# Hybrid decoder step: paged keys turned on VectorE in 32x32 blocks, and the projection tiles reordered around it

## The reference

```python
k_full = k_pages[pt_b[:n_full * ppb]].reshape(n_full, M_BLOCK, M_HEADS, M_DH)
means = jnp.mean(k_full.astype(jnp.float32), axis=1).swapaxes(0, 1)
idx, valid = moba_select(qh, means, n_full_q, k_sel)      # best 3 of 4 blocks of 256
...
return moba_core(qh, kg, vg, valid, k_own, v_own, own_mask)   # softmax over them and the own tokens
```

## Time and profile before

| What | Value |
|---|---|
| Median of 3 runs | 1973.92 us (1972.58 to 1979.55) |
| Profiled execution, span from first to last instruction | 1972.4 us |
| Median less span | 1.5 us |
| TensorE busy | 1951.0 us, 99% |
| VectorE busy | 1269.6 us, 64% |
| ScalarE busy | 881.4 us, 45% |
| POOL busy | 145.1 us, 7% |
| Granted TensorE clock | 0.999 of full speed |
| DMA traffic | 267 MB, mean 135 GB/s |

### The profile page before, as it was taken

One profiled execution on the slowest core, in us unless ns is written; L12 is line 12 of the kernel. 1 busy time (PEld: TensorE's weight loads), 2 busy tenths in 40 slices (PEclk: granted clock), 3 DMA queues, 4 the chain that ended last, 5 costly groups with the idle time before them and its releaser, 6 DMA issues. The chain is left out here.

```text
span 1972.4 us, 40938 instructions
## 1 busy us (share of the span) xinstructions
PE 1951.0 (99%) x16779; PEld 1829.6 (93%) x16779; DVE 1269.6 (64%) x2022; ACT 881.4 (45%) x1423; POOL 145.1 (7%) x231
## 2 busy tenths in 40 slices
PE   9999999999999999999999999999999999999999
PEld 8968978998999999999998798799899999999999
DVE  6475413347765988988674743143686658889876
ACT  4365522323534454655434754233334344555544
POOL 0001120012000000000000012200120000000000
PEclk9999999999999999999999999999999999999999
DMA  6327683246244343333343277812552442433332
GB/s 214 124 69 221 203 283 103 86 148 205 89 153 132 86 132 97 97 108 91 102 157 131 86 215 236 286 52 91 171 163 90 157 139 71 136 104 107 87 113 83
DMA packets 262059, 267.12 MB, mean 135 GB/s; under 512 B 14026, under 2 KB 225138, under 8 KB 261362
## 3 DMA queue, kind: packets, MB, share of 16 engines
q1 hardware_dynamic: 241522, 190.69, 31.3%
q0 software_dynamic: 20224, 73.68, 11.5%
q10 hardware_dynamic: 128, 0.15, 0.0%
HBM read 239.43 MB, written 25.03 MB: 134 GB/s over the span
## 5 line engine op out<-in xcount | busy, mean ns | idle before, releaser
L1999 DVE TENSOR_TENSOR WL<-RAW,WH 128x2048 fp32r<-128x2048 f32 (+2 forms) x76 | 161.1, 2120 | 93.0 <-ACT WH L1428 93.0
L856 PE MATMUL PS<-XH,WH 128*128 128x272 f32 x960 | 203.3, 293 | 0.6
L856 PE MATMUL PS<-XL,WH 128*128 128x272 f32 x960 | 198.3, 288 | 0.0
L856 PE MATMUL PS<-XH,WL 128*128 128x272 f32 x960 | 198.0, 287 | 0.0
L1334 PE MATMUL PS<-KQ,CH 128*128 128x272 f32 x1088 | 158.3, 288 | 1.4 <-DVE KQ L2552 1.4
L1428 ACT ACTIVATE WH<-RAW 128x2048 fp32r<-128x2048 f32 (+2 forms) x84 | 149.8, 1783 | 21.8 <-PE PS L856 19.1
L856 PEld LDWEIGHTS PS<-XH,WH 128*128 128x128 f32 x960 | 150.5, 188 | 7.8 <-issue 5.2
L836 PE MATMUL PS<-WH,XH 128*128 128x256 f32 x512 | 152.1, 297 | 0.0
L856 PEld LDWEIGHTS PS<-XL,WH 128*128 128x128 f32 x960 | 150.9, 188 | 0.0
L856 PEld LDWEIGHTS PS<-XH,WL 128*128 128x128 f32 x960 | 150.3, 189 | 0.0
L1334 PEld LDWEIGHTS PS<-KQ,CH 128*128 128x128 f32 x1088 | 145.0, 188 | 2.2 <-issue 2.2
(11 more groups left out here) (464 smaller groups left out, 5266.8 us busy)
## 6 DMA issues: line engine op xcount, KB each, us to landing
RAW<-in_w_in SPq DMA_DIRECT2D x94, 512.0 KB, 4.7
RAW<-in_w_gu SPq DMA_DIRECT2D x128, 256.0 KB, 3.8
PG<-in_cache_k SPq DMA_DIRECT2D x64, 256.0 KB, 3.3
PG<-in_cache_k POOLq DMA_DIRECT2D x64, 256.0 KB, 3.4
RAW<-in_w_down SPq DMA_DIRECT2D x64, 256.0 KB, 4.0
RAW<-in_w_gu SPq DMA_DIRECT2D x24, 512.0 KB, 4.6
PG<-in_cache_v SPq DMA_DIRECT2D x44, 256.0 KB, 3.9
PG<-in_cache_v POOLq DMA_DIRECT2D x44, 256.0 KB, 4.2
```

The lines of the kernel that those rows point to most:

```text
L856: last = pe.matmul(PS[:, 2 * pair + h, 0:HALF], w[:, i, c0:c0 + P], block[:, h * HALF:(h + 1) * HALF], start=first and i == 0 and a == 0, ...
L1999: dve.tensor_tensor(WL[:, slot, 0:n], RAW[:, slot, 0:n], WH[:, slot, 0:n].bitcast(F32), ALU.subtract).then_inc(lo_ready, 1)
```

## The change

Key pages are no longer turned on TensorE. Each page is fetched by four DMAs of 64 KB. DMA g takes features 128g to 128g + 127 of all 128 tokens and puts token 32c + k on partition 32g + k, for the four c side by side. One VectorE instruction (`dve.transpose`) then turns every 32x32 block of a page number's four pages (128 x 2048) in place. The contraction over features now takes four products with 32 features of each of the four bands, so the sample queries have their columns in another order (`sample_pairs`), and `QB` is made by eight-head masked products on VectorE (`query_block`) from a new constant `qmask`. `KTT`, its copies and POOL's memset of `QB` go.

There are four key buffers (two `PG`, a part of `XT`, and `PGK` where the attention operand `MT` was) and three of them serve the values. `rqk` is cut: its first unit (`rqa`) stays in the attention stage, with tile 3 now there and tile 4 ahead of the first scores; the `rv` tiles fill the key stage; the other three units (`rqb`) fill the value stage. Scores and probabilities of the two groups use different PSUM banks.

```diff
+    PAGE_BUFS = (PG[:, 0], PG[:, 1], XT[:, 4:8, 0:SEQ], PGK[:])
@@ pages
+            v = r - V_STEP
+            if r == 2:
+                hold(eng, xt_kept, lay * 16 + 16)
+            elif r == 3:
+                hold(eng, s_done, lay * 16 + 16)
+            elif 4 <= r < V_STEP:
+                hold(eng, sc_done, scores_done(lay, r - 4))
+            elif 0 <= v < 3:
+                hold(eng, sc_done, scores_done(lay, V_STEP - 4 + v))
             for b in seqs:
-                if r >= V_STEP + 3:
-                    hold(eng, pvs_page, lay * 64 + 4 * (r - V_STEP - 3) + b + 1)
...
-                elif r >= 2:
-                    hold(eng, kt_done, lay * 64 + 4 * (r - 2) + b + 1)
+                if v >= 3:
+                    hold(eng, pvs_page, lay * 64 + 4 * (v - 3) + b + 1)
                 e = (r // N_PAGES % 2 * GRP + b) * N_PAGES + r % N_PAGES
                 page = eng.value_load(PTAB[0:1, e:e + 1], min_val=0, max_val=cache_k.shape[1] - 1)
...
+                src = src.rearrange("o n (c k) h d -> k (o n c) (h d)", k=32)
+                for g in range(4):
+                    dst = key_buf(r)[32 * g:32 * g + 32, b, :].rearrange("k (c d) -> k c d", c=4)
+                    eng.dma_start(dst, src[:, :, g * P:(g + 1) * P]).then_inc(arrived[r % 4], 16)
@@ SP
-                for at_r, name, j, col in ((2, "rqk", 2, C_RQ), (6, "rqk", 3, C_RQ), (11, "rv", 0, C_RV),
-                                           (14, "rv", 1, C_RV), (20, "rv", 2, C_RV), (23, "rv", 3, C_RV),
-                                           (27, "br_att", 0, C_GA)):
+                for at_r, name, j, col in ((4, "rv", 1, C_RV), (7, "rv", 2, C_RV), (10, "rv", 3, C_RV),
+                                           (14, "rqb", 0, C_RQ + UC), (18, "rqb", 1, C_RQ + UC),
+                                           (21, "rqb", 2, C_RQ + UC), (25, "br_att", 0, C_GA)):
@@ TensorE, end of the prompt attention
                 if s == 16:
-                    turn_keys(0, (0,))
+                    token_part("rqa", 3, kk[:4])
                 if s:
                     turn_probs(s - 1)
             attend(14)
-            turn_keys(0, (1,))
+            token_part("rqa", 3, kk[4:])
             attend(15)
@@ key_scores
-                pe.wait_ge(kt_act, lay * 64 + 4 * q + 4)
+                pe.wait_ge(kt_turned, lay * 16 + q + 1)
...
-                for hp in range(4):
+                for e in range(4):
                     for b in range(GRP):
-                        last = pe.matmul(PS[32 * b:32 * b + 32, 4 + p // 4, (p % 4) * P:(p % 4 + 1) * P],
-                                         QB[:, hp, (g * GRP + b) * 32:(g * GRP + b + 1) * 32],
-                                         KTT[q % 2][:, b, hp, :], start=hp == 0, stop=hp == 3)
+                        keys = key_buf(q)[:, b, :].rearrange("p (c e k) -> p c e k", c=4, e=4)[:, :, e, :]
+                        last = pe.matmul(PS[32 * b:32 * b + 32, (4, 0)[g] + p // 4, (p % 4) * P:(p % 4 + 1) * P],
+                                         QB[:, e, (g * GRP + b) * 32:(g * GRP + b + 1) * 32],
+                                         keys, start=e == 0, stop=e == 3)
@@ TensorE, key and value stage
+            token_part("rqa", 4, kk)
+            for q in range(V_STEP):
+                for f in value_rows(q):
+                    token_part("rv", f, kk)
+                key_scores(q)
+                if q == 11:
+                    turn_sample_probs(0)
+            for i in range(V_STEP):
+                g, p = divmod(i, N_PAGES)
+                if i == 0:
+                    token_part("rv", 4 * TT - 1, kk)
+                for f in late_rows(i):
+                    token_part(*rq_tile(f), kk)
+                if i == 4:
+                    turn_sample_probs(1)
+                attend_sample(g, p)
+                if i == 9:
+                    to_columns(0)
@@ VectorE
+            def query_block(j):
+                dve.wait_ge(tr_done, lay * 16 + j + 1)
+                q = PS[:, QK_BANKS[j % 3][1], 0:NS].rearrange("p (b q) -> p b q", q=DEC_L)
+                w = cl("qmask")[:, j // 2 * 8:j // 2 * 8 + 8]
+                dve.tensor_tensor(QB[:, j, :].rearrange("p (b h q) -> p b h q", b=DEC_B, q=DEC_L),
...
+            def turned(r):
+
+                dve.wait_ge(page_in[r % 4], key_landings(lay, r))
+                dve.wait_ge(page_in_b[r % 4], key_landings(lay, r))
+                dve.transpose(key_buf(r), key_buf(r)).then_inc(kt_turned, 1)
@@ VectorE, prompt attention (after the scaling of step s and row_max(s + 2))
+                if s in (8, 10, 12):
+                    turned(s // 2 - 4)
@@ VectorE, key stage
             rotated(2)
-            for q in range(NG * N_PAGES):
+            split_at(U0["rv"])
+            rotated(3)
+            turned(3)
+            rotated(4)
+            for q in range(V_STEP):
+                if q in (1, 5, 9, 13):
+                    split_at(U0["rv"] + (q + 3) // 4)
+                if 4 <= q + 3 < V_STEP:
+                    turned(q + 3)
                 if q == N_PAGES:
                     select(0)
```

More of the change, by code:

```diff
@@ L430, in diag, with key_buf, slot_total, key_landings @@
         return bass.AP(a.tensor, a.offset + 0, [list(a.ap[0]), [256, 4], [36, 8], [1, 4]])
-    def own_query(hp, z):
-        return QB[64 * z:64 * z + 64, hp, :].rearrange("p (b c) -> p b c", c=32)[:, :, 8 * hp + 4 * z:8 * hp + 4 * z + 4]
-    def page_slot(r):
-        if r < V_STEP:
-            used = [r % 2 == q % 2 for q in range(r)]
-            return r % 2, PG[:, r % 2], sum(used), V_STEP // 2 + len(range(r % 2, V_STEP, 3))
-        slot, before = (r - V_STEP) % 3, (r - V_STEP) // 3
-        keys = V_STEP // 2 if slot < 2 else 0
-        buf = PG[:, slot] if slot < 2 else PGE[:]
-        return slot, buf, keys + before, keys + len(range(slot, V_STEP, 3))
+    def key_buf(q):
+        return PAGE_BUFS[q % 4]
+    def slot_total(slot):
+        return V_STEP // 4 * KEY_PIECES + 32 * len(range(slot, V_STEP, 3))
+    def key_landings(lay, q):
+        return lay * (slot_total(q % 4) if q % 4 < 3 else V_STEP // 4 * KEY_PIECES) + (q // 4 + 1) * KEY_PIECES
+    def value_slot(lay, v):
+        slot = v % 3
+        return slot, PAGE_BUFS[slot], lay * slot_total(slot) + V_STEP // 4 * KEY_PIECES + (v // 3 + 1) * 32
+    def scores_done(lay, q):
+        return lay * 18 + q + 1 + (q >= N_PAGES)
     def row_bank(name, f):
-        if name == "rqk" and f < 2:
+        if name == "rqa" and f < 2:
             return 1, slice(f * UC, (f + 1) * UC)
-        return (3, 6)[f % 2], slice(0, UC)
+        if name == "rqa" and f == 3:
+            return 2, slice(0, UC)
+        return (3, 6)[(T0[name] + f - T0["rqa"]) % 2], slice(0, UC)
     QK_BANKS = ((4, 5), (6, 7), (2, 3))
@@ L463, in out_pair, with value_rows, late_rows @@
         return (0, 2, 6, 4, 0)[t]
-    def value_tiles(g, p):
-        step, out = g * N_PAGES + p, []
-        for r in ((0, 1) if step == 0 else (step + 1,) if step + 1 < 4 * (TT - 1) else ()):
-            u, i = divmod(r, TT - 1)
-            out += [u * TT, u * TT + 1] if i == 0 else [u * TT + 1 + i]
-        return out
-    def filler(q):
-        return q + 3 if q < N_PAGES else q + 5
+    def value_rows(q):
+        return [q - 1 + u for u in range((q + 3) // 4 - (q % 4 == 1), (q + 3) // 4 + 1)] if q else []
+    VALUE_STEPS = (1, 2, 3, 5, 6, 7, 8, 10, 11, 12, 13, 14)
+    def late_rows(i):
+        if i not in VALUE_STEPS:
+            return []
+        n = VALUE_STEPS.index(i)
+        return [TT + n // 4 * TT] * (n % 4 == 0) + [TT + n // 4 * TT + 1 + n % 4]
     def out_bank(h):
@@ L832, in token_part @@
                 if t == TT - 1:
-                    last = sample_part(u, bank, (0, 1) if len(ks) == KT else (ks[0] // 4,))
+                    last = sample_part(slot, bank, (0, 1) if len(ks) == KT else (ks[0] // 4,))
                 for k in ks if t < TT - 1 else ():
@@ L878, in unit2, with transposes @@
                 feature_tile(tile + 1, 2 * slot + 1, slot, UC, P, kts, rhs)
-            def transposes(srcs, base, pairs, between):
+            def transposes(srcs, base, pairs, between, sample=None):
                 w = len(pairs)
@@ L892, in transposes @@
                         else:
-                            pe.matmul(PS[:, bank, 0:NS], src(t), STK, start=True, stop=True).then_inc(tr_done, 1)
+                            rows = src(t) if sample is None else sample(j)
+                            pe.matmul(PS[:, bank, 0:NS], rows, STK, start=True, stop=True).then_inc(tr_done, 1)
                     between(j)
@@ L927, in sample_rkv, with sample_columns @@
                     last.then_inc(rs_done, 1)
-            transposes([rows_of(QK, j) for j in range(8)], 0, QK_BANKS, sample_kv)
+            def sample_columns(j):
+                return QK[:, TT - 1, j * P:(j + 1) * P]
+            transposes([rows_of(QK, j) for j in range(8)], 0, QK_BANKS, sample_kv, sample_columns)
```

(10 more changed lines are left out.)

323 lines of the change are left out of this document (135 added, 188 removed).

## The result

The change makes the kernel slower: 1985.62 us median of 12 runs (1978.34 to 1989.96) against 1973.96 of 12 runs before (1972.42 to 1979.55), a ratio of 1.0055 with a 95% interval from 1.0043 to 1.0066. The forecast was 1950, with a range up to 1976.

What follows compares the result with a forecast made beforehand. TensorE, busy 99%, bounds the kernel before; key-page supply was to bound the changed key stage. Saving 2.0 there and 9.7 in the value stage, 23.4 us over both layers, takes the 1972.4 span to 1949.0, so 1950 (range 1926 to 1976).

Steps and rivals of the forecast that it cites:

- Transposes off TensorE, turning at 2.3 us: All 512 TensorE transposes go, at most 56 us in both layers; VectorE turns each page in 2.3 us instead.
- Rival B: On VectorE, turning takes twice the split, 4.6 us, costing 7 us a layer: 1964 us; chance 0.13.
- Attention stage: Three turnings inserted in VectorE's attention loop cost 4.0 us (bounds 0 and 6.9); last attention product ends at 154.1.
- Page 0's release: Key stage start: page 0 is scored by 161.5 us, and only then may page 4 be issued.
- Supply of 5.8 us a page: Key stage: the queues issue a page in 5.8 us (bounds 5.0 and 7.3), over TensorE's 4.1; scores end at 236.8.
- break-even of 6.8 us a page: Key-page issue: the change turns from gain to loss at 6.8 us a page.
- Bandwidth has room as well: Key stage DMA: 512-byte rows move 297 GB/s at a full share, while a page with its weights asks 233.
- D: Key stage: issuing a piece costs POOL 0.756 us, a page 7.2, 17 us more a layer: 1984 us; chance 0.08.
- E: Key-page DMA: pieces writing only 32 partitions run at half of 297 GB/s, 40 us more a layer: 2030; chance 0.05.
- Value stage: Value stage takes 65 us instead of 74.7, saving 9.7 a layer (bounds 1.5 and 11.3).
- Rival C: The value stage is bound by its transfers and saves only 1.5 us: 1966 us; chance 0.14.
- Slower: Whole kernel slower by more than the 10 us a measurement can tell, the cases D and E; chance 0.13.

Runs made afterwards that it cites:

- e5: Changed kernel with the turnings of pages 0 to 2 moved from VectorE's attention loop to behind its last step: 1975.55 us.
- e9: e5 with TensorE scoring pages 0, 1 and 2 directly behind the last attention product, ahead of the fifth retention tile: 1958.16 us.
- e6: Changed kernel with VectorE's block selection of group 0 moved ahead of the turning of page 9, from behind that of page 11: 1989.0 us.
- e7: Changed kernel with 12 idle TensorE products ahead of the wait for each turned page from page 4 on, except page 8: 1997.02 us.
- e8: Changed kernel with four of the 16 pieces of each of pages 4 to 15 issued by ScalarE's queue: 1982.91 us.
- e2: Changed kernel with one 256 KB DMA per key page of a sequence, in 512-byte runs, without placing the feature bands: 1953.55 us.
- e11: Changed kernel with two 128 KB pieces per key page of a sequence, whole rows to 64 neighbouring partitions each, without placing the feature bands: 1967.27 us.
- e12: Changed kernel with two 128 KB pieces per key page of a sequence, half the columns to all 128 partitions each, without placing the feature bands: 1944.4 us.
- e16: e11 with one piece writing the even and the other the odd partitions, instead of the first and last 64: 1947.43 us.
- e13: e9 plus ScalarE's queue sharing the pieces of pages 6 to 15 (1949.64 us), then block selection moved ahead of page 10's turning: 1944.48 us.
- e3: Changed kernel with its four 64 KB pieces cut by blocks of 32 keys, each writing all 128 partitions and a quarter of the columns: 2080.9 us.

## Why the prediction was wrong

- **Transposes off TensorE, turning at 2.3 us.** Right: 512 instructions fewer, and 2.308 us for a turning. That is what the split takes for as many elements (2.29). The trace agrees so far with the Trainium skill's page "Vector Engine (DVE) Microarchitecture Reference", section 3.8, by which a transposing pass sustains one element per cycle per lane. Rival B is out.
- **Attention stage.** The mechanism was right, the term 2 us short: 156.1 instead of 154.1. The three insertions were priced at 4.0; e5, which takes them out of the loop, ends at 150.4, so they cost 5.7. VectorE's small gaps took nothing back.
- **Page 0's release.** Forecast 161.5, found 166.3 (164.93 + 1.40). Of the 4.8 us, 2 are the attention's. The pause before the fifth tile was forecast well, at 3.3 us, and found at 3.42, although the rotation that it was reckoned from ends at 151.09 (150.80 + 0.29) and not at 150.80. The rest is a thing that the forecast had nowhere. Behind that pause, in the fifth tile, TensorE's products stand 0.21 us apart instead of 0.12, the 1.2 GHz level instead of 2.4 (granted clock 0.50 from 160 to 164 us, 1.00 from 150 to 156 and again from 167 to 171). Windows, then the timeline:

```profile
150.00:156.00 6.00, 6.00 (x64) 5.31 (x60) 0.00 (x0) 1.45 (x2) 0.00 (x0) 1.00 0.55 166
160.00:164.00 4.00, 4.00 (x21) 4.00 (x21) 2.99 (x9) 2.27 (x2) 0.00 (x0) 0.50 0.02 4
167.00:171.00 4.00, 4.00 (x60) 3.73 (x56) 2.89 (x7) 1.19 (x3) 2.53 (x5) 1.00 0.46 131
```

```profile
159.54 0.55 PE L868 MATMUL PS<-WH,XH 128*128 128x256 f32 x1 [3.42 <-ACT EA L1468]
159.89 0.41 PE L869 MATMUL PS<-WL,XH 128*128 128x256 f32 x1
160.10 0.41 PE L870 MATMUL PS<-WH,XL 128*128 128x256 f32 x1
...
167.35 0.28 PE L869 MATMUL PS<-WL,XH 128*128 128x256 f32 x1
167.47 0.28 PE L870 MATMUL PS<-WH,XL 128*128 128x256 f32 x1
```

  The tile took 5.4 us (159.54 to 164.93) instead of 3.08. Page 0's scores then took 1.40 us instead of 1.01. In the kernel before, the pause at this place was 1.51 us and the clock stayed at 1.00 (150 to 156 us). In the changed kernel the clock fell again later: from 196 to 200 us TensorE was busy 1.50 us of 4, and from 200 to 205 the granted clock was 0.68. e9, in which the fifth tile waits only 0.65 us and page 0 is released first, shows what an early release is worth: 17.4 us.
- **Supply of 5.8 us a page.** This is the step that failed: 12 x 5.8 from 161.5, and 1.9 for the landing. The suspect was right, but its terms were too small. The scores of layer 0 end at 251.5 instead of 236.8, 14.7 us late:

| Term | Forecast | Found | Adds |
|---|---|---|---|
| Page 0's release | 161.5 | 166.3 | 4.8 |
| From the release to POOL's first piece of page 4 | 0 | 1.3 | 1.3 |
| Issue of twelve pages on POOL | 69.6 | 75.6 | 6.0 |
| From the end of the issue to the last landing | 1.9 | 4.65 | 2.7 |
| Turning, last scores, own keys | 3.8 | 3.65 | -0.1 |

  The issue was too small because a page takes POOL 6.05 without pauses (the forecast had 5.5 for POOL) and because of the pauses. The one of 2.40 us comes after the first piece that POOL issues for page 14. It is as long and at the same piece in e5, e6, e7 and e9, so TensorE's waits, which differ there, do not make it; what does was not found. By the forecast's own break-even of 6.8 us a page, POOL's 6.30 would still have left a small gain, so the loss needed the release and the landing too.

  The landing was too small because of "Bandwidth has room as well", which took 297 GB/s at a full share from a window with 512-byte rows. That window's transfers did not have this kernel's shape. The changed kernel's move 251 at a full share, and its pieces land 2.4 to 4.6 us after issue (medians by buffer and queue from 168 to 230 us) instead of 1.9.

  On average the engines still had room, at a share of 0.85. So POOL's issue paces the changed kernel, as the same 75.6 us in e9 say too. The transfers and the order of work stand close behind it, as e8 shows, so that shortening the issue alone gave 2.7 us. What one DMA to all partitions gives, 32.1 us (e2), comes from issue and transfer together, and no run splits it for pieces of 64 KB.

  The score stage of layer 1 is 5.2 us longer than that of layer 0 (100.6 and 95.4). POOL took 78.5 us for the twelve pages there, 3.0 more than in layer 0; why, and where the rest comes from, is not explained.
- **The rivals.** D's time, 1984, is close to the result by accident: a piece cost POOL about 0.59 us, not 0.756, and the rest of the loss is terms that D did not have. E had a mechanism that the runs show for pieces of 128 KB (e11 against e12 and e16), at 5% and with too large a size. It is there in the changed kernel's 251 GB/s, but how much of the 14.7 us it makes was not measured. The other rule that the forecast named, of the Trainium skill's page "DMA: Bandwidth & Descriptors" against transfers under 64 KB, is not needed for the slowness of e11, as 128 KB pieces were slow there and fast in e12 and e16; for the 64 KB pieces of the changed kernel no run tests it.
- **Value stage.** Right: 65 forecast, 65.0 and 66.0 found. Rival C is out.
- **The chances.** "Slower" had 0.13. The range's upper end, 1976, left out exactly the two rivals in which the new DMAs cost more than a plain row of the trace said, though no row showed a DMA of their shape. The sign of being wrong that was named for them, a period of issue over 6.8, did not appear: the kernel lost with 6.30.

## What to carry to other kernels

Price a new DMA by what it looks like: how many pieces, how long the runs, and how many partitions one piece reaches; two pieces to the first and last 64 partitions cost 27 us over one DMA, two by columns or by even and odd partitions 4 to 7. Where buffers are recycled, the stage lasts from the first release to the last landing, so look for the work that can release the first buffer sooner: that was worth 17 us here without a byte less. Try an order change again after the bound has moved; nearly the same move was worth nothing in e6 and 5 us in e13.

## What had not been expected of the hardware

- The same two DMAs of 64 partitions took 1967.3 as halves and 1947.4 as even and odd partitions (e11, e16).
- SP took 1.11 us to issue a piece of 128 runs of 512 bytes to 128 partitions, and 0.64 for as many runs in 32 partitions (e3, after).
- TensorE's products ran 0.21 us apart behind a wait of 3.42 us, at a granted clock of 0.50, and 0.12 apart again from 167.35 us on, at 1.00.
